# Norms carried over the stage boundaries, three steps moved inside the mixers, and key stacks requested by ScalarE

## The reference

```python
h = rms_norm(x, attn_norm[l]);  proj = h @ w_in[l]
o_fox  = fox_attention(...)      # 6 heads of 64, forget gates
o_diff = diff_attention(...)     # 4 heads, two score maps each, q and k of 32
o_dsa  = dsa_attention(...)      # 6 heads of 64, keys kept by a top-128 index score
x = x + concatenate([o_fox, o_diff, o_dsa]) @ w_out[l]
h = rms_norm(x, ffn_norm[l]);  gate, up = split(h @ w_gate_up[l])
x = x + (silu(gate) * up) @ w_down[l]
```

## Time and profile before

| | us |
|---|---|
| median of three runs | 2142.5 (2140.75 to 2143.71) |
| profiled execution | 2137.17 |
| its span, first to last instruction | 2135.4 |
| PE busy | 1959.8 (92%) |
| DVE busy | 1199.1 (56%) |
| ACT busy | 849.8 (40%) |
| POOL busy | 523.1 (24%) |

### The profile page before, as it was taken

The page is one execution under the profiler, slowest core; times in us unless marked ns, Lnnn a source line. Parts: engine busy times, 40 slices in busy tenths (PEclk is TensorE's granted clock), DMA queues, the critical chain, the costliest instruction groups (busy, mean ns, idle before and its releaser), DMA issues. The chain is left out here.

```text
span 2135.4 us, 30252 instructions
## 1 busy us (share of the span) xinstructions
PE 1959.8 (92%) x11384; PEld 1702.9 (80%) x11384; DVE 1199.1 (56%) x2338; ACT 849.8 (40%) x1402; POOL 523.1 (24%) x447
## 2 busy tenths in 40 slices
PE   6898898999999989899899999998999989799994
PEld 6798887888888879888788888878888879677773
DVE  3765765444543466567544444469932233498885
ACT  4345554222211344455431222133234452277772
POOL 2565421000000246552100000016544444200001
PEclk9999998999999999999899999999999999799997
DMA  4112323313211111232233313116647732689995
GB/s 164 43 58 80 95 85 128 119 60 118 107 70 59 47 58 60 70 105 65 89 121 116 118 59 118 59 69 129 102 131 226 239 135 109 245 331 400 405 411 209
DMA packets 73533, 288.80 MB, mean 135 GB/s; under 512 B 18240, under 2 KB 23104, under 8 KB 48960
## 3 DMA queue, kind: packets, MB, share of 16 engines
q1 hardware_dynamic: 61456, 243.61, 33.2%
q10 hardware_dynamic: 9360, 34.08, 4.5%
q0 software_dynamic: 2592, 9.44, 1.2%
HBM read 244.14 MB, written 37.19 MB: 132 GB/s over the span
## 5 line engine op out<-in xcount | busy, mean ns | idle before, releaser
L1299 PE MATMUL fill_ps<-w_hi,h_hi 128*128 128x256 f32 (+1 forms) x704 | 209.0, 297 | 14.0 <-PEq L3169 5.1
L1299 PE MATMUL fill_ps<-w_hi,h_lo 128*128 128x256 f32 (+1 forms) x704 | 203.3, 289 | 0.0
L1299 PE MATMUL fill_ps<-w_lo,h_hi 128*128 128x256 f32 (+1 forms) x704 | 203.0, 288 | 0.0
L322 POOL TENSOR_SCALAR norm_ss<-norm_ss 128x1 f32<-128x1 f32 x24 | 4.8, 201 | 797.0 <-ACT ffn_raw_d L316 739.6
L845 POOL TENSOR_TENSOR w_lo<-w_raw,w_hi 128x512 fp32r<-128x512 f32 x120 | 160.9, 1365 | 144.7 <-ACT w_hi L913 144.5
L516 DVE TENSOR_TENSOR ffn_silu<-ffn_silu,ffn_up 128x512 f32<-128x512 f32 x44 | 30.2, 687 | 286.4 <-ACT ffn_silu L474 286.4
L1796 POOL TENSOR_TENSOR w_lo<-w_raw,w_hi 128x512 fp32r<-128x512 f32 x96 | 145.0, 1539 | 138.4 <-ACT w_hi L1880 134.7
L474 ACT ACTIVATE ffn_silu<-ffn_up 128x512 f32<-128x512 f32 x44 | 26.3, 598 | 337.0 <-PE ffn_up L575 336.9
L528 DVE TENSOR_TENSOR x<-ffn_down,x 128x512 f32<-128x512 f32 x176 | 119.1, 688 | 71.3 <-PE ffn_down L590 70.4
L1299 PEld LDWEIGHTS fill_ps<-w_hi,h_hi 128*128 128x128 f32 x704 | 139.8, 199 | 23.5 <-issue 17.9
L575 PE MATMUL ffn_up<-h_hi,w_hi 128*128 128x512 f32 x384 | 152.1, 396 | 3.3 <-PEq L792 3.3
(11 more groups left out here) (454 smaller groups left out, 5320.2 us busy)
## 6 DMA issues: line engine op xcount, KB each, us to landing
moe_raw_gu<-in_w_e_gu SPq DMA_DIRECT2D x46, 1024.0 KB, 11.4
w_raw<-in_w_mix SPq DMA_DIRECT2D x28, 1024.0 KB, 5.1
w_raw<-in_w_two SPq DMA_DIRECT2D x23, 1024.0 KB, 5.9
moe_raw_d<-in_w_e_down SPq DMA_DIRECT2D x23, 1024.0 KB, 7.9
w_raw<-in_w_gate SPq DMA_DIRECT2D x22, 1024.0 KB, 5.3
w_raw<-in_w_up SPq DMA_DIRECT2D x22, 1024.0 KB, 6.7
ffn_raw_d<-in_w_down SPq DMA_DIRECT2D x22, 1024.0 KB, 4.8
moe_in<-in_zero ACTq DMA_DIRECT2D x23, 512.0 KB, 5.2
```

Of the source, the lines that this page charges most:

```text
L322: self.core.nc.gpsimd.tensor_scalar(s_t, s_t, 1.0 / D, NORM_EPS, ALU.mult, ALU.add).then_inc(self.rooted, 1)
L1299: last = nc.tensor.matmul(b[:, 0:cols], aw[:, k, t * P:(t + 1) * P], ww[:, k, 0:cols], start=k == 0 and n == 0, stop=k == KD - 1 and n == 2)
```

## The change

1. **Carried norms.** A stage now norms only row blocks 0 and 1 completely; of block 2 it makes square and root. A new class `LateNorm` makes the rest inside the next stage: the `hi` and `lo` of block 1 (its transposes stay in PSUM across the barrier, in `turn_ps`), scaling, transposes, `hi` and `lo` of blocks 2 and 3, and square and root of block 3. The slots and gain rows lie in tiles that last over all stages (`fqk`, `sqk`). In a mixer the transposes stand behind the products of row blocks 0 and 1 of chunk 0. In a feed-forward the first group's gate and up products are cut in halves of 256 columns (`up_by_halves`), the first half ahead of the carried blocks. This holds for loading to mixer, mixer to feed-forward (twice) and feed-forward to mixer; the last feed-forward (`cut` false) ends as before.
2. **Moved steps in the mixers.** GpSimd splits half a chunk ahead of the second and third root and half behind. VectorE takes the third sum of squares and normalisation two search rounds earlier. Unit 18 moves from step 51 to 53. The exponential for the differential heads' factor on ACT moves two evictions back.
3. **Key stacks.** ACT issues the four key requests of each of the eight pairs (`stack_keys`); SyncE issues the four query requests, and waits for the query unit alone.

Line numbers of the new kernel differ. The diff, cut to what matters:

```diff
...
+class LateNorm:
...
+    def half(self, t, h):
+        bank = (self.held[h] if t == 1 else self.banks[2 * (t - 2) + h])[:].rearrange("p (k n) -> p k n", n=P)
+        cut = (slice(None), slice(4 * h, 4 * h + 4), slice(t * P, (t + 1) * P))
+        return bank, self.core.h_hi[cut], self.core.h_lo[cut]
...
+    def square(self, act):
+        t = TB - 1
+        self.core.nc.scalar.activation(self.core.norm_slots[t % 2], self.core.x[:, t, :], ACT.Square,
...
+    def turn(self, pe, t):
+        pe.wait_ge(self.scaled, t - 1)
+        if t == TB - 1:
+            pe.wait_ge(self.lo_done, 2)
...
+                        sp.wait_ge(late.turned, 4)
+                        sp.dma_start(core.norm_rows, w_down(g)).then_inc(down_in, 16)
...
+                late.root(pool)
...
                         act.wait_ge(up_sum, 2 * HB * (g - 1))
                     split(g, s, 0, gate_in)
+                    if isinstance(g, int) and g == 0:
+                        late.hi(act, 1)
+                        late.square(act)
                     split(g, s, 1, up_in)
+                    if isinstance(g, int) and g == 0:
+                        late.hi(act, 2)
+                        late.hi(act, 3)
                     if not (isinstance(g, int) and g == 0):
                         hidden(g - 1, 1 - s)
...
+                    if isinstance(g, int) and g == 0:
+                        late.scale(dve, 2)
+                        late.lo(dve, 1)
+                        late.scale(dve, 3)
...
+                def up_by_halves():
+                    first, rest = slice(0, 2 * P), slice(2 * P, 4 * P)
+                    of = [((gu_hi[0][m], hi), (gu_lo[0][m], hi), (gu_hi[0][m], lo)) for m in range(2)]
+                    pe.wait_ge(late.hi_done, 2)
+                    part(0, 0, first, of[0][:2], True, False)
+                    late.turn(pe, 2)
+                    pe.wait_ge(late.lo_done, 2)
+                    part(0, 0, first, of[0][2:], False, True)
+                    late.turn(pe, 3)
+                    part(0, 1, first, of[0], True, True)
+                    pe.wait_ge(lo_done, 1)
+                    for b in range(HB):
+                        part(1, b, first, of[1], True, True)
+                    pe.wait_ge(late.lo_done, 6)
                     for b in range(HB):
                         for m in range(2):
-                            if b == 0 and not (isinstance(g, int) and g == 0 and m == 0):
+                            part(m, b, rest, of[m], True, True).then_inc(up_sum, 1)
...
-UNIT_AT = {4: 4, 5: 5, 8: 6, 9: 7, 12: 8, 13: 9, 16: 10, 17: 11, 19: 12, 21: 13, 26: 14, 28: 15, 44: 16, 45: 17, 51: 18, 56: 19}
+UNIT_AT = {4: 4, 5: 5, 8: 6, 9: 7, 12: 8, 13: 9, 16: 10, 17: 11, 19: 12, 21: 13, 26: 14, 28: 15, 44: 16, 45: 17, 53: 18, 56: 19}
...
-                    sp.wait_ge(unit_lo, max(qu, ku) + 1 if e < 2 * DIFF else qu + 1)
+                    sp.wait_ge(unit_lo, qu + 1)
...
-                        for half, (q_m, k_m) in enumerate(((u_hi, u_hi), (u_lo, u_hi), (u_hi, u_lo), (u_lo, u_lo))):
+                        for half, q_m in enumerate((u_hi, u_lo, u_hi, u_lo)):
                             copy_rows(e, stack[2 * (e % 2)], half, q_m[q], slice(r0, r1))
-                            copy_rows(e, stack[2 * (e % 2) + 1], half, k_m[k], slice(r0, r1))
                     else:
...
+                late.root(pool)
+                for h in range(2):
+                    split_lo(1, h)
+                pool.wait_ge(late.scaled, 2)
...
-                for p in range(3):
+                norm_root(0)
+                for h in range(2):
+                    split_lo(3, h)
+                for p in range(1, 3):
+                    split_lo(p + 3, 0)
                     norm_root(p)
-                    for h in range(2):
-                        split_lo(p + 3, h)
+                    split_lo(p + 3, 1)
...
+                def stack_keys(e):
+                    _, ku, r0, r1 = head_units(DIF0 + e)
+                    act.wait_ge(unit_lo, ku + 1)
+                    if e >= 2:
+                        act.wait_ge(scored, TB * (DIF0 + e - 1))
+                    for half, k_m in enumerate((u_hi, u_hi, u_lo, u_lo)):
+                        act.dma_start(stack[2 * (e % 2) + 1][stack_rows_of(half, slice(r0, r1)), :].bitcast(F32),
+                                      k_m[UNIT_SLOT[ku]][r0:r1, :].bitcast(F32)).then_inc(stacked[e % 2], 16)
+
...
+                late.hi(act, 1)
+                late.square(act)
                 for h in range(2):
                     split_hi(1, h)
+                late.hi(act, 2)
...
-                        if c == 0 and t == 0:
+                        if c == 0 and t == 1:
+                            late.hi(act, 3)
...
+                    for pair in range(2 * DIFF):
+                        if stack_step(pair) + (pair + 1 if pair < 2 else 0) == n:
+                            stack_keys(pair)
...
-                for t in range(TB):
+                for t in range(TB - 1):
                     act.wait_ge(added, 8 * (MIX_OUT - 1) + 2 * t + 2)
                     norm.square(act, t)
-                    if t >= 1:
-                        norm.hi(act, t - 1)
-                norm.hi(act, TB - 1)
+                    if t == 1:
+                        norm.hi(act, 0)
...
+                late.scale(dve, 2)
+                late.lo(dve, 1)
+                late.scale(dve, 3)
+                late.lo(dve, 2)
+                late.lo(dve, 3)
...
                     find(r)
+                    if r == 1:
+                        sum_squares(2)
                     take(r)
                     if r == 0:
                         normalise(1, 0)
-                    if r == 3:
-                        sum_squares(2)
-                    if r == 4:
...
+                        if c == 0 and t >= 1:
+                            pe.wait_ge(late.lo_done, 2 * t)
...
+                        if c == 0 and t < 2:
+                            late.turn(pe, t + 2)
...
-                for t in range(1, TB):
-                    norm.turn(pe, t)
+                norm.turn(pe, 1)
...
+            core.turn_ps = [core.psum(f"turn_ps{b}", [P, SEQ], carried) for b in range(4)]
+            core.norm_rows = core.sqk[:].rearrange("p t d -> p (t d)")
+            core.norm_slots = [core.norm_rows[:, n * D:(n + 1) * D] for n in range(2)]
+            core.gains = [core.fqk[:].rearrange("p t h d -> p (t h d)")[:, n * D:(n + 1) * D] for n in range(2)]
...
-                for t in range(TB):
+                for t in range(TB - 1):
                     norm.root(pool, t)
 
             @block.scalar
             def _(act):
-                for t in range(TB):
+                for t in range(TB - 1):
                     act.wait_ge(x_in[t], 16)
                     norm.square(act, t)
-                    if t >= 1:
-                        norm.hi(act, t - 1)
-                norm.hi(act, TB - 1)
+                    if t == 1:
+                        norm.hi(act, 0)
+                act.wait_ge(x_in[TB - 1], 16)
...
```

150 lines of the change are left out of this document (98 added, 52 removed).

## The result

| | before | after |
|---|---|---|
| median of the timed runs | 2142.4 us (4 runs, 2140.8 to 2143.7) | **2121.9 us** (4 runs, 2118.7 to 2125.5) |
| ratio, 95% interval | | 0.9905 (0.9885 to 0.9926) |
| profiled execution | 2137.2, span 2135.4 | 2119.5, span 2117.7 |

The change brings 20.5 us, and I had forecast 44.3: 2098.2, with a range that ended at 2117. Timed again in a later session, the changed kernel came to 0.9878 (0.9854 to 0.9901) of the kernel before.

What follows compares the result with a forecast made beforehand. TensorE was taken as the bound: its waits, its added work and its clock (0.50 or 1.00). Terms -3.8 - 17.4 - 9.5 + 8.0 - 3.0 - 11.4 - 7.2 = -44.3 us gave 2098.2 us, range 2085 to 2117.

Steps and rivals of the forecast that it cites:

- Start of the kernel: Kernel start: first products from 19.2, 6.0 us earlier, less 2.2 for added transposes; term -3.8 us.
- Front of each mixer: Start of both mixers: `w_lo` waits -2.55, third normalisation -3.35, clock -2.2, first score -0.6; -8.7 us each, -17.4 together.
- The rival in which VectorE takes the front back: Mixer fronts: VectorE idled 5.02 us, the front gains 8.7, so 3.7 could return per mixer; 2106 us, chance 0.10.
- my 12.5: First mixer's first score: expected 12.5 us earlier than before.
- near 90: First mixer: time on the new axis at which the first score was expected, written beside -12.5.
- Key halves, first pair: First stacks of both mixers: ACT issuing key requests cuts 2.5 us of waiting each, plus clock 1.7 and 2.8; -9.5 together.
- The sum 190.4 + 4 requests + 2.1 us of landing: First pair: ACT's key requests from 190.4, last starting at 192.3 and landing at 194.4; wait becomes 0.6 us.
- Key halves, ACT's price: ACT's queue, both mixers: key requests delay what is queued behind, 4.0 us each, +8.0, with 0 and 40 as ends.
- the six pairs that I called covered by idle time: Six of each mixer's eight pairs: ACT's idle time takes most of the requests' delay, 0.9 us in sum.
- Unit 18: Its transpose two steps later in each mixer: TensorE resumes at 259.65 instead of 261.70; -1.5 us each, -3.0 together.
- Both stage boundaries: Mixer to feed-forward, twice: -5.7 us each, -11.4; feed-forward to second mixer, once: -7.2.
- the -8: Mixer to feed-forward: alternative term if half-width products cost hardly more than whole ones, about -8 us instead of -5.7.

## Why the prediction went wrong

**Start of the kernel: right.** First product at 19.42 (I said 19.2). The cast started at 14.88.

**Front of each mixer: right in sum, wrong in its parts.** -8.7 forecast, about -8 and -7 measured. That is one execution's: the changed kernel's profile has a stretch at 0.50 from 65.0 to 68.4 that the kernel before has not, and it leads by 11.5 us at step 8; five of the profiled kernels with the same front run there at 1.00 and lead by 13.7 to 14.1. The `w_lo` waits are 1.3 per mixer and not gone: I had one of the halves ready 0.2 us before it is needed, and TensorE, which has lost its longer wait, is there sooner than it. For that TensorE comes later to the second unit's transpose and waits 0.2 us there and not 1.4. The clock behind the place is 1.00 as I had it. The rival in which VectorE takes the front back is out: VectorE's first maximum came only 7.7 us earlier, but at step 8 the lead is 11.5. The first score came at 97.3, 11.5 earlier; my 12.5 would have put it at 96, and the "near 90" that I wrote beside it was a slip.

**Key halves, first pair: the step that failed.** I had the first stacks' waits at 0.6 and 1.2 us; they were 4.3 and 4.0. The sum 190.4 + 4 requests + 2.1 us of landing holds when nothing is in the way, and a run measured its 0.6 us. It used the landing time of copies that had the DMA engines to themselves. My own working named each queue that the change shortens, and did not ask what stands next in it. It was 1 MB of weights, 20 us earlier than before, of which 11.5 are the kernel's lead. Off by 11 us over two mixers.

**Key halves, ACT's price: a little under-sized.** 8.0 forecast; by the maxima 5.2 and 4.4 us in the changed kernel, 9.6, and 11.2 where the chunk is out of the way, of which some 2 us are a stretch at 0.50 that falls elsewhere in other executions. In waits alone it is 7.1. The request's duration and the wait of unit 17 (1.7 forecast, 1.3 measured) were right; I had too little for the six pairs that I called covered by idle time, where waits of 0.2 to 1.2 us for the transposed probabilities and the exponential add up.

**Unit 18: the step failed.** TensorE resumed where I had it, but I counted as gain the transposes and the half speed that only come later. The forecast needed the wait to become shorter, and it stayed: 3.7 us before, 3.5 after, both behind the same row of VectorE's work. -3.0 forecast, no difference measured.

**Both stage boundaries: right.** From the end of block 1's transposes (338.87) to the end of the up products (366.74 - 1.41 = 365.33) it took 26.5 us (26.7 forecast), 0.12 per product of half width at clock 1.00. The Trainium skill's figure for the load ("TensorE: Matmul & The Clock Gate", "LDWEIGHTS (loading the stationary operand)") would have given the -8, and the trace does not show it. The second mixer starts 0.3 us behind the last transpose.

**Feed-forward bodies: a term I did not have.** 6.6 us through where tiles lie. The diff shows it: two tiles that were local to the mixer are now opened ahead of everything, and the feed-forward's up weights behind them move by 20864 bytes, away from the offset of the activations that they are multiplied with.

With the last, the first-pair and the unit-18 terms at what the runs showed, the forecast would have been 2098.2 + 6.6 + 11.0 + 3.0 = 2118.8, and with ACT's 9.6 for 8.0 it would have been 2120.4, inside the measured 2118.7 to 2125.5. With executions that scatter by 5 us this sum is a check of the order, not a proof of each term.

## To carry to other kernels

When requests leave a queue, write down what stands behind them in it: it moves up too, and if it is large it meets the very transfers that were to come sooner. Before a second engine is set to issuing, try whether the first engine can issue in two goes; here that shortened the first stacks' wait from 6.1 to 3.1 us, where 1.1 was in reach, without the price of the requests on ACT. And when a change alters which tiles live where, compare the interval of identical products before and after, by tile: 3% of it needs no wait to appear in any list. A wait that a moved step leaves behind goes to the next thing in the same engine's queue, so read that queue and not the step; and work that is moved behind a wait is not saved, it is still to be done.
